# Softmax weights of layers 1 and 2: division by the sums moved from an activation into the product that turns them

## The chip, the cores and the metric

One Trainium2 chip, one of its cores. The metric is the device time of one launch in microseconds (us). The time of the kernel before is 1606.17 us, the median of 3 runs (1606.01 to 1606.25).

The engines of the core go by these names in the profile: PE (TensorE, matrix products; PEld is its loading of the stationary operand), ACT (ScalarE), DVE (VectorE), POOL (GpSimd) and SP (SyncE, which issues most of the DMA).

## The reference

The program computes, for 256 tokens of width 1024, two "hybrid" layers and then two layers of another block (gated feed-forwards, a neighbourhood attention with an mLSTM scan, a spatial gating). The change touches only the first two layers, and there the attention. Each layer has 16 heads of width 64: eight (group 0) with a causal mixture of three dilated windows, eight (group 1) with plain causal attention.

```python
def hybrid_layer(x, c, cos, sin, pre_g, post_g, w_ada, b_ada, w_in, w_out):
    shift, scale, gate = jnp.split(silu(c) @ w_ada + b_ada, 3, axis=-1)
    h = rms_norm(x, pre_g) * (1 + scale) + shift
    qa, ka, va, ga, qb, kb, vb, gb = jnp.split(h @ w_in, ...)
    ...
    o_a = merge(dilated_mixture_attention(qa, ka, va)) * silu(ga)   # softmax over causal windows
    o_b = merge(moba_attention(qb, kb, vb)) * silu(gb)              # softmax, causal
    y = concatenate([o_a, o_b]) @ w_out
    return x + gate * rms_norm(y, post_g)
```

For 256 tokens both attentions come down to, for each head, P = exp(S - max), each row divided by its own sum, and then P times V. The second block's first layer also has a context of 256 tokens, whose normalization (rms_norm of ctx, "cx0" in the kernel) is prepared at the end of layer 2.

## The kernel before, in words

Everything stays on the core. Weights stream from HBM in 428 tiles of 256 x 512; SP issues the transfers in an order fixed ahead, into a ring of slots. Each weight tile is split on the way into a high part (ACT, `act_tick`, a copy of 128x1024 to `sb_hi`) and a low part (DVE, `dve_tick`, a difference of 128x1024 to `sb_w..r`), and PE makes three products per tile and token block (high x high, high x low, low x high), each 128x512 or 128x256. Splits run three to seven tiles ahead of PE. DVE also makes the modulation vectors out of further tiles (`dve_vector`, 128x1024 each).

The order on each engine is written out by hand. Layer l has units u = 0 to 39, one weight tile each: q, k, v and q again of the two head groups, k, v, the gates (units 24 to 31), then the output projection (32 to 39). The table `B1` hangs further work on units: `("A", v)` and `("B", v)` are step v of the attention of group 0 and 1, and `("tq", g)`, `("tk", g)` are the turning of q and k. Step v of the attention does on PE (`pe_attention`) the following: turn head 2v-2 (`pe_turn`), weigh the two heads before (`pe_weigh`, P times V), scores of heads 2v and 2v+1 (`pe_scores`), turn head 2v-1. Steps lie about two units apart. A head's scores are 128x128 for its first 128 queries and 128x256 for its last.

The way of a pair of heads before the change is: PE scores into a bank; DVE adds the mask and finds the maxima (`dve_scores`); ACT takes the exponential, with the sum as its accumulator (`act_exp`, sums into `stat[..., 2:4]`); DVE takes the reciprocals of four sums at once (`dve_sums`, the item `"r"`); ACT multiplies the weights by them, in place, one 128x128 and one 128x256 activation for each head (`act_shares`); PE turns the three 128x128 blocks by transposes against the identity `ident` (`pe_turn`; it waits for the signal "share"); ACT copies the 128x384 out of the bank (`act_weights`); PE weighs.

POOL is nearly idle in these layers: it makes the 1/sqrt of the norms (`pool_rstd`, a power of -0.5 on one or two columns) and the low parts of some of the normalized rows (`pool_low`). `pool_norm(e, "cx0")` does so for the context. On DVE, `("cxn", i)` is the normalization of half i of the context and `("cx", i)` its further steps; PE turns it in `pe_norm(e, "cx0", ...)` when its own order comes to `("cx", i)`.

Of the kernel before, what the change touches and what calls it, by code (L numbers as in the profile page):

```python
# [353 lines left out]
def build(nc, I, out):  # L354
    ctx = ExitStack()
    with ctx:
# [64 lines left out]
        minus_half, kk2 = sb("minus_half", [128, 8]), sb("kk2", [128, 32])  # L421
        crow, ones = sb("crow", [1, 1024], at=xc_at), sb("ones", [1, 128], at=xc_at + 4096)
# [74 lines left out]
        def done(s, *what):  # L497
            return s, s.of(*what)
# [443 lines left out]
        def split_ready(*key):  # L942
# [12 lines left out]
              for g in range(2)]  # L955
        y = XN
# [17 lines left out]

        for v in range(4):
            for l in range(2):
                B1[l].setdefault(((16, 18, 20, 22), (11, 13, 15, 17))[l][v], []).insert(0, ("r", (0, v)))
                B1[l].setdefault(((25, 27, 29, 31), (23, 25, 27, 29))[l][v], []).insert(0, ("r", (1, v)))
# [142 lines left out]
        def pe_turn(e, l, g, h):  # L1121
            b = BANK["P", l, g, h] = HB3.take()
            for f in b.free():
                e.wait_ge(*f)
            e.wait_ge(*done(AE, "share", l, g, h))
            for x in range(3):
                m = e.tr(b.ap[:, x * 128:(x + 1) * 128], PB[h % 3][:, x * 128:(x + 1) * 128], ident)
            m.then_inc(TRP.sem, TRP.put("P", l, g, h))
            b.till = ((AE, "PT", l, g, h),)
# [37 lines left out]
        def act_shares(e, l, g, v):  # L1167

            e.wait_ge(*done(DE, "recip", l, g, v))
            for h in (2 * v, 2 * v + 1):  # L1170
                r, p = stat[:, l, g, h, :], PB[h % 3]
                e.act(p[:, 0:128], p[:, 0:128], ACT.Copy, scale=r[:, 2:3]).then_inc(AE.sem, AE.put("share", l, g, h, 0))
                e.act(p[:, 128:384], p[:, 128:384], ACT.Copy, scale=r[:, 3:4]).then_inc(AE.sem, AE.put("share", l, g, h))

# [34 lines left out]
        def dve_sums(e, l, g, v):  # L1209

            r = stat[:, l, g, 2 * v:2 * v + 2, 2:4]
            e.wait_ge(*done(EX, l, g, 2 * v + 1))
            e.recip(r, r).then_inc(DE.sem, DE.put("recip", l, g, v))
# [53 lines left out]
        def act_block1(e, l):  # L1267
# [18 lines left out]
            for u in range((35, 38)[l]):  # L1286
# [30 lines left out]
                for what, i in B1[l].get(u, ()):  # L1317
                    if what == "r":
                        act_shares(e, l, *i)
# [40 lines left out]
        def dve_block1(e, l):  # L1360
# [25 lines left out]
            for u in range((35, 38)[l]):  # L1386
                for what, i in B1[l].get(u, ()):
                    if what == "r":
                        dve_sums(e, l, *i)
# [100 lines left out]
        def pool_block1(e, l):  # L1490
            if l == 1:
                pool_rstd(e, "cx0")
                pool_norm(e, "cx0")
# [29 lines left out]

        def act_conditions(e):

            e.wait_ge(*done(LD["cb2"], 2))
            for n in range(4):
                c = slice(n % 2 * 512, n % 2 * 512 + 512)
                e.act(SG[n][:, :], CB[1 + n // 2][:, c], ACT.Tanh, scale=0.5).then_inc(AE.sem, AE.put("cb", 1 + n // 2, n % 2))

        def dve_conditions(e):

            for n in range(4):
                z = CB[1 + n // 2][:, n % 2 * 512:n % 2 * 512 + 512]
                e.wait_ge(*done(AE, "cb", 1 + n // 2, n % 2))
                e.stt(z, SG[n][:, :], 1.0, z, ALU.add, ALU.mult).then_inc(DE.sem, DE.put("cb", 1 + n // 2, n % 2))
# [42 lines left out]
        def pool_start(e):  # L1579
            e.memset(ones[:, :], 1.0).then_inc(PO.sem, PO.put("ones"))  # L1580
            e.memset(minus_half[:, :], -0.5).then_inc(PO.sem, PO.put("minus_half"))
            pool_rstd(e, "a0")
# [1523 lines left out]
```

## Time and profile before

| | |
|---|---|
| median of 3 runs | 1606.17 us (1606.01 to 1606.25) |
| the profiled execution | 1606.1 us, with a span of 1604.3 us from the first to the last instruction and 1.8 us around it |
| mean granted TensorE clock | 0.999 |
| PE busy | 1575.7 us, 98% of the span |
| PEld busy | 1311.9 us, 82% |
| DVE busy | 1173.6 us, 73% |
| ACT busy | 792.1 us, 49% |
| POOL busy | 70.4 us, 4% |

Times in the rows below are us from the start of the span. The attention of layer 1 lies between about 62 and 141 us, that of layer 2 between about 196 and 279 us. Durations of neighbouring matmuls overlap in the records, so for PE the distance from start to start is the time that a group takes.

### The profile page before, as it was taken

Reading aid. Unit: us, or ns where it says so; the run is one execution under the profiler, and the core shown is the slowest. Engines: PE = TensorE matmul, PEld = TensorE weight load, DVE = VectorE, ACT = ScalarE, POOL = GpSimd, SP = SyncE. Lnnn points to the kernel's source line nnn. Section 1 sums busy time; section 2 is a strip of 40 time slices with the busy share of each in tenths; the row PEclk is TensorE's granted clock in tenths of the full one; section 3 lists DMA queues with packets and bytes.
Section 4 is the critical chain, followed back from the end, with each engine's and each line's share of the span. In section 5 each row is a group of like instructions: output and inputs, shape, how many; then the busy total and the mean of one; then the engine's idle time right before and its main releaser. Section 6 shows DMA issues by size and latency. Waiting matters only on the chain.

```text
span 1604.3 us, 20979 instructions
## 1 busy us (share of the span) xinstructions
PE 1575.7 (98%) x8098; PEld 1311.9 (82%) x8098; DVE 1173.6 (73%) x1925; ACT 792.1 (49%) x1298; POOL 70.4 (4%) x112
## 2 busy tenths in 40 slices
PE   7999999999999999999999999999999999999998
PEld 5787778888888888887777888888888888888887
DVE  8899888759876665477755799868887667666654
ACT  5877677432221222254555555535554553455542
POOL 2000000100000000030010100000000100010000
PEclk9999999999999999999999999999999999999999
DMA  9987665336656664252131688766777585555550
GB/s 378 358 321 276 232 237 180 124 107 247 210 210 223 227 219 173 90 173 79 66 99 66 236 313 305 287 242 243 275 269 260 214 309 195 171 197 186 189 182 35
DMA packets 93046, 336.99 MB, mean 210 GB/s; under 512 B 10625, under 2 KB 11265, under 8 KB 92690
## 3 DMA queue, kind: packets, MB, share of 16 engines
q1 hardware_dynamic: 90706, 327.58, 56.6%
q0 software_dynamic: 2240, 8.06, 1.5%
q8 instruction: 64, 1.05, 0.3%
q14 instruction: 36, 0.29, 0.1%
HBM read 334.56 MB, written 1.05 MB: 209 GB/s over the span
## 4 chain that ended last, share of the span: by engine, by line
PE 54%; DVE 2%; issue 1%; ACT 0%; POOL 0%; POOLq 0%; DVEq 0%; ACTq 0%
PE bank L292 53%; PE bank L295 2%; DVE sb_tm L301 0%; DVE sb_XN L309 0%; DVE sb_XN L301 0%; DVE sb_X L301 0%; DVE sb_arena L312 0%; DVE sb_arena L319 0%; ACT sb_XN L298 0%; DVE sb_sg L316 0%; DVE sb_XC L301 0%; DVE sb_w8r L301 0%; DVE sb_w5r L301 0%; POOL sb_rstd L301 0%; DVE sb_arena L309 0%
## 5 line engine op out<-in xcount | busy, mean ns | idle before, releaser
L292 PE MATMUL bank<-sb_hT,sb_hi 128*128 128x512 f32 (+1 forms) x1856 | 574.7, 379 | 0.0
L298 ACT ACTIVATE sb_hi<-sb_w 128x1024 fp32r<-128x1024 f32 x428 | 432.0, 1052 | 286.1 <-DMA sb_w<-in_w 235.2
L292 PEld LDWEIGHTS bank<-sb_hT,sb_hi 128*128 128x128 f32 x1856 | 332.1, 188 | 58.5 <-issue 0.2
L292 PE MATMUL bank<-sb_hi,sb_hT 128*128 128x512 f32 x1152 | 369.6, 395 | 2.7 <-ACT sb_hT L298 1.3
L292 PEld LDWEIGHTS bank<-sb_hi,sb_hT 128*128 128x128 f32 x1152 | 215.6, 188 | 53.1 <-issue 5.3
L312 DVE CUSTOM_DVE_ANT_0 sb_w<-sb_w,sb_cb 128x1024 f32<-128x1024 f32 x144 | 174.9, 1219 | 0.0
L301 DVE TENSOR_TENSOR sb_sg<-bank,sb_sg 128x512 f32<-128x512 f32 (+1 forms) x90 | 58.8, 660 | 97.5 <-ACT sb_sg L298 78.0
L298 ACT ACTIVATE sb_sg<-bank 128x512 f32<-128x512 f32 (+1 forms) x98 | 55.0, 574 | 120.2 <-PE bank L292 120.0
L301 DVE TENSOR_TENSOR sb_tm<-bank,sb_rows 128x512 f32<-128x512 f32 (+1 forms) x41 | 28.1, 684 | 71.8 <-PE bank L292 68.9
L298 ACT ACTIVATE sb_arena<-bank 128x512 f32<-128x512 f32 (+1 forms) x106 | 56.2, 556 | 46.6 <-PE bank L292 32.5
L298 ACT ACTIVATE sb_XN<-sb_X 128x512 f32<-128x512 f32 x33 | 20.7, 629 | 99.7 <-DVE sb_X L301 92.7
L301 DVE TENSOR_TENSOR sb_w0r<-sb_w,sb_hi 128x1024 fp32r<-128x1024 f32 x43 | 52.3, 1217 | 18.6 <-ACT sb_hi L298 18.6
L301 POOL TENSOR_TENSOR sb_rstd<-sb_rstd,sb_minus_half 128x1 f32<-128x1 f32 (+1 forms) x23 | 14.1, 613 | 1174.7 <-DVE sb_rstd L309 1174.7
L298 ACT ACTIVATE sb_arena<-sb_arena,sb_stat 128x128 f32<-128x128 f32 (+1 forms) x128 | 52.2, 446 | 26.0 <-DVE sb_stat L312 26.0
L312 DVE CUSTOM_DVE_ANT_0 sb_w<-sb_w,sb_rows 128x1024 f32<-128x1024 f32 x48 | 57.7, 1221 | 0.3 <-ACT sb_rows L298 0.3
L301 DVE TENSOR_TENSOR sb_w3r<-sb_w,sb_hi 128x1024 fp32r<-128x1024 f32 x42 | 51.2, 1219 | 7.9 <-ACT sb_hi L298 7.7
L301 DVE TENSOR_TENSOR sb_w2r<-sb_w,sb_hi 128x1024 fp32r<-128x1024 f32 x39 | 47.8, 1226 | 10.7 <-ACT sb_hi L298 10.7
L301 DVE TENSOR_TENSOR sb_w1r<-sb_w,sb_hi 128x1024 fp32r<-128x1024 f32 x39 | 47.5, 1218 | 8.4 <-ACT sb_hi L298 8.4
L301 DVE TENSOR_TENSOR sb_w5r<-sb_w,sb_hi 128x1024 fp32r<-128x1024 f32 x36 | 43.9, 1220 | 10.2 <-ACT sb_hi L298 10.2
L312 DVE CUSTOM_DVE_ANT_0 sb_tmw<-sb_w,sb_cb 128x1024 f32<-128x1024 f32 x40 | 48.8, 1220 | 0.4
L295 PE MATMUL bank<-sb_cst,sb_arena 128*128 128x128 f32 x256 | 39.2, 279 | 8.6 <-ACT sb_arena L298 7.4
L292 PE MATMUL bank<-sb_hT,sb_w0r 128*128 128x256 f32 (+1 forms) x152 | 47.4, 321 | 0.0
(486 smaller groups left out, 3244.3 us busy)
## 6 DMA issues: line engine op xcount, KB each, us to landing
sb_w<-in_w SPq DMA_DIRECT2D x428, 512.0 KB, 4.3
sb_w<-in_mw SPq DMA_DIRECT2D x192, 512.0 KB, 4.9
sb_rows<-in_na_rpb POOLq DMA_DIRECT2D x16, 96.0 KB, 3.4
sb_X<-in_x SPq DMA_DIRECT2D x1, 1024.0 KB, 4.9
sb_cb<-in_cvec POOLq DMA_DIRECT2D x2, 512.0 KB, 9.4
sb_XC<-in_ctx POOLq DMA_DIRECT2D x1, 1024.0 KB, 13.2
sb_arena<-in_sg_ln_g POOLq DMA_DIRECT2D x1, 1024.0 KB, 5.9
sb_arena<-in_sg_ln_b POOLq DMA_DIRECT2D x1, 1024.0 KB, 9.1
```

What stands on the lines that cost most here:

```text
L292: return self.e.matmul(out, a, b, start=start, stop=stop)
L295: return self.e.transpose(out, a, ident)
L298: return self.e.activation(out, a, f, **kw)
L301: return self.e.tensor_tensor(out, a, b, op)
L312: return self.e.tensor_tensor_reduce(out=out, in0=a, in1=b, scale=scale, scalar=init, op0=op0, op1=op1, accum_out=accum)
```

## The change

Per pair of heads, the reciprocal leaves DVE and the two times two scaling activations leave ACT. In their place POOL raises the four sums to the power -1 (against a new constant `minus_one`), and then fills for each head a buffer `SHARE` of two 128x128 squares: the identity times the head's two columns of shares, that is, squares whose diagonal holds 1/sum (one for the first 128 queries, one for the last). `pe_turn` no longer transposes against `ident`; it multiplies each block of weights with its square, as an ordinary f32 product, so that the turned block comes out divided. `SHARE` has room for two heads and lies in `SG[3]`; a fill waits for the turn of the head two before. `SG[3]` was scratch for one of the four `tanh` of the conditions, which now uses half a row block of `XN`. Besides, the normalization of the context's second half, `("cxn", 1)`, moves from unit 34 to unit 33 of layer 2, and POOL's `pool_rstd(e, "cx0")` goes between the third and the fourth pair of group 0 in layer 2.

```diff
-               34: [("gate", 0), ("cxn", 1)], 35: [("cx", 2), ("cx", 3)]}]
+               33: [("cxn", 1)], 34: [("gate", 0)], 35: [("cx", 2), ("cx", 3)]}]
...
-        for v in range(4):
-            for l in range(2):
-                B1[l].setdefault(((16, 18, 20, 22), (11, 13, 15, 17))[l][v], []).insert(0, ("r", (0, v)))
-                B1[l].setdefault(((25, 27, 29, 31), (23, 25, 27, 29))[l][v], []).insert(0, ("r", (1, v)))
...
-            e.wait_ge(*done(AE, "share", l, g, h))
+            e.wait_ge(*done(PO, "share", l, g, h))
             for x in range(3):
-                m = e.tr(b.ap[:, x * 128:(x + 1) * 128], PB[h % 3][:, x * 128:(x + 1) * 128], ident)
+                m = e.mm(b.ap[:, x * 128:(x + 1) * 128], PB[h % 3][:, x * 128:(x + 1) * 128],
+                         SHARE[:, h % 2, min(x, 1), :], True, True)
...
-        def act_shares(e, l, g, v):
-
-            e.wait_ge(*done(DE, "recip", l, g, v))
-            for h in (2 * v, 2 * v + 1):
-                r, p = stat[:, l, g, h, :], PB[h % 3]
-                e.act(p[:, 0:128], p[:, 0:128], ACT.Copy, scale=r[:, 2:3]).then_inc(AE.sem, AE.put("share", l, g, h, 0))
-                e.act(p[:, 128:384], p[:, 128:384], ACT.Copy, scale=r[:, 3:4]).then_inc(AE.sem, AE.put("share", l, g, h))
...
-        def dve_sums(e, l, g, v):
+        def pool_shares(e, l, g, v):
 
             r = stat[:, l, g, 2 * v:2 * v + 2, 2:4]
             e.wait_ge(*done(EX, l, g, 2 * v + 1))
-            e.recip(r, r).then_inc(DE.sem, DE.put("recip", l, g, v))
+            e.tt(r, r, minus_one.rearrange("p (h j) -> p h j", h=2), ALU.pow).then_inc(PO.sem, PO.put("sums", l, g, v))
+            for h in (2 * v, 2 * v + 1):
+                if h > 1:
+                    e.wait_ge(*done(TRP, "P", l, g, h - 2))
+                elif g:
+                    e.wait_ge(*done(TRP, "P", l, 0, 6 + h))
+                e.wait_ge(*done(PO, "sums", l, g, v))
+                e.tt(SHARE[:, h % 2, :, :], ident.unsqueeze(1).to_broadcast([128, 2, 128]),
+                     stat[:, l, g, h, 2:4].unsqueeze(2).to_broadcast([128, 2, 128]), ALU.mult).then_inc(
+                    PO.sem, PO.put("share", l, g, h))
...
         def pool_block1(e, l):
+            e.wait_ge(*done(PO, "minus_one"))
+            for g in range(2):
+                for v in range(4):
+                    if (l, g, v) == (1, 0, 3):
+                        pool_rstd(e, "cx0")
+                    pool_shares(e, l, g, v)
             if l == 1:
-                pool_rstd(e, "cx0")
                 pool_norm(e, "cx0")
```

On PE, at the second step of the attention in layer 1 (`sb_arena` holds the weights, the scores' operands and the like; `sb_cst` is the identity, `sb_sg_85` is `SG[3]`, the squares; the moving operand is named first), before and now:

```order
 L292 MATMUL bank<-sb_hi_72,sb_hT 128x512
-L295 MATMUL bank<-sb_cst,sb_arena 128x128 x3
+L292 MATMUL bank<-sb_sg_85,sb_arena 128x128 x3
 L292 MATMUL bank<-sb_arena 128x128 x2
 L292 MATMUL bank<-sb_arena 128x256 x2
-L295 MATMUL bank<-sb_cst,sb_arena 128x128 x3
+L292 MATMUL bank<-sb_sg_85,sb_arena 128x128 x3
 L292 MATMUL bank<-sb_hi_73,sb_hT 128x512
```

Each group of three transposes has become three products in the same place; nothing else has moved on PE. There are 32 such groups, 96 instructions.

On POOL, in layer 2, between the end of layer 1's low parts (`sb_hT`) and the power for the context (`sb_rstd`, 128x2), and behind it:

```order
 L301 TENSOR_TENSOR sb_hT<-sb_sg_85,sb_hT 128x2x128
+L301 TENSOR_TENSOR sb_stat<-sb_stat,sb_minus_one 128x2x2
+L301 TENSOR_TENSOR sb_sg_85<-sb_cst,sb_stat 128x256 x2
...
 L301 TENSOR_TENSOR sb_rstd<-sb_rstd,sb_minus_half 128x2
+L301 TENSOR_TENSOR sb_stat<-sb_stat,sb_minus_one 128x2x2
+L301 TENSOR_TENSOR sb_sg_85<-sb_cst,sb_stat 128x256 x2
```

POOL's queue has gained, over both layers, 16 powers of four columns and 32 fills of 128x256, in this pattern.

On DVE, at the end of layer 2 (`sb_XN<-sb_XC` is the normalization of the context's second half, the others are low parts of weight tiles):

```order
 L301 TENSOR_TENSOR sb_w0r<-sb_w_49,sb_hi_75 128x1024
 L301 TENSOR_TENSOR sb_w8r<-sb_w_65,sb_hi_76 128x1024
+L305 TENSOR_SCALAR sb_XN<-sb_XC,sb_rstd 128x512 x2
 L301 TENSOR_TENSOR sb_w1r<-sb_w_51,sb_hi_71 128x1024
 L301 TENSOR_TENSOR sb_w4r<-sb_w_57,sb_hi_72 128x1024
-L305 TENSOR_SCALAR sb_XN<-sb_XC,sb_rstd 128x512 x2
```

It now stands two low parts earlier. ACT has lost 64 activations and DVE 16 reciprocals; both keep the order of the rest.

## Rows read from the trace of the kernel before

**Rows 1.** The page: span and busy time of each engine

```profile
span 1604.3 us, 20979 instructions
PE 1575.7 (98%) x8098; PEld 1311.9 (82%) x8098; DVE 1173.6 (73%) x1925; ACT 792.1 (49%) x1298; POOL 70.4 (4%) x112
```

**Rows 2.** Waits of PE, 0 to 330 us: total us, times, longest

```profile
PE bank L295 <- ACT sb_arena L298: 7.4, 11, 1.6
```

**Rows 3.** Timeline of PE: turns that waited (start, us, idle before)

```profile
70.31 0.52 PE L295 MATMUL bank<-sb_cst,sb_arena 128*128 128x128 f32 x3 [0.16 <-ACT sb_arena L298]
...
135.62 0.52 PE L295 MATMUL bank<-sb_cst,sb_arena 128*128 128x128 f32 x3 [1.17 <-ACT sb_arena L298]
...
218.53 1.39 PE L295 MATMUL bank<-sb_cst,sb_arena 128*128 128x128 f32 x11 [0.45 <-ACT sb_arena L298]
...
274.29 0.52 PE L295 MATMUL bank<-sb_cst,sb_arena 128*128 128x128 f32 x3 [1.32 <-ACT sb_arena L298]
```

**Rows 4.** Timeline of PE: eight transposes and the product behind them

```profile
183.13 1.04 PE L295 MATMUL bank<-sb_cst,sb_arena 128*128 128x128 f32 x8
183.92 0.48 PE L292 MATMUL bank<-sb_hi,sb_hT 128*128 128x512 f32 x1
```

**Rows 5.** Timeline of PE: eight f32 products (16 records), mLSTM stage

```profile
764.75 1.95 PE L292 MATMUL bank<-sb_arena,sb_tm 128*128 128x128 f32 x16
766.45 0.48 PE L292 MATMUL bank<-sb_hi,sb_hT 128*128 128x512 f32 x1
```

**Rows 6.** Timeline of PE: eight f32 products against the identity (gate rows)

```profile
140.92 2.05 PE L292 MATMUL bank<-sb_cst,sb_mods 128*128 128x128 f32 x16
142.73 0.47 PE L292 MATMUL bank<-sb_hi,sb_yT0h 128*128 128x512 f32 x1
```

**Rows 7.** Groups of POOL with shapes: busy us, mean ns, idle before

```profile
L301 POOL TENSOR_TENSOR sb_hT<-sb_sg,sb_hT 128x256 fp32r<-128x256 f32 x28 | 21.8, 778 | 61.9 <-ACT sb_hT L298 61.9
L301 POOL TENSOR_TENSOR sb_rstd<-sb_rstd,sb_minus_half 128x1 f32<-128x1 f32 x20 | 11.1, 553 | 1121.4 <-DVE sb_rstd L309 1121.4
L301 POOL TENSOR_TENSOR sb_mlhr<-sb_mlhr,sb_minus_half 128x8 f32<-128x8 f32 x1 | 1.7, 1674 | 0.1
```

**Rows 8.** Timeline of DVE and POOL: one power alone, one beside DVE

```profile
217.13 0.70 POOL L301 TENSOR_TENSOR sb_rstd<-sb_rstd,sb_minus_half 128x2 f32<-128x2 f32 x1 [44.27 <-DVE sb_rstd L309]
...
686.57 1.22 DVE L301 TENSOR_TENSOR sb_w1r<-sb_w,sb_hi 128x1024 fp32r<-128x1024 f32 x1
686.73 1.63 POOL L301 TENSOR_TENSOR sb_rstd<-sb_rstd,sb_minus_half 128x2 f32<-128x2 f32 x1 [2.17 <-DVE sb_rstd L309]
```

**Rows 9.** Timeline of DVE and POOL around 290 us

```profile
289.29 1.52 POOL L301 TENSOR_TENSOR sb_hT<-sb_sg,sb_hT 128x512 fp32r<-128x512 f32 x1 [71.46 <-ACT sb_hT L298]
290.19 1.70 DVE L301 TENSOR_TENSOR sb_w8r<-sb_w,sb_hi 128x1024 fp32r<-128x1024 f32 x1 [0.51 <-ACT sb_hi L298]
```

**Rows 10.** Timeline of ACT and DVE: exponentials' ends, and one pair's neighbours

```profile
67.38 0.19 ACT L298 ACTIVATION_READ_ACCUMULATOR sb_arena<-sb_arena,sb_stat 128x1 f32 x1
...
132.21 0.19 ACT L298 ACTIVATION_READ_ACCUMULATOR sb_arena<-sb_arena,sb_stat 128x1 f32 x1
134.68 1.49 ACT L298 ACTIVATE sb_arena<-sb_arena,sb_stat 128x128 f32<-128x128 f32 x4
...
269.62 0.19 ACT L298 ACTIVATION_READ_ACCUMULATOR sb_arena<-sb_arena,sb_stat 128x1 f32 x1
...
132.15 1.22 DVE L312 CUSTOM_DVE_ANT_0 sb_w<-sb_w,sb_rows 128x1024 f32<-128x1024 f32 x1
133.38 1.19 DVE L301 TENSOR_TENSOR sb_w3r<-sb_w,sb_hi 128x1024 fp32r<-128x1024 f32 x1
```

**Rows 11.** Groups of DVE, 55 to 332 us

```profile
L322 DVE RECIPROCAL sb_stat<-sb_stat 128x4 f32<-128x4 f32 x16 | 2.8, 177 | 6.7 <-ACT sb_arena L298 6.7
```

**Rows 12.** Timeline of PE: first turn of the context's second half

```profile
294.71 1.29 PE L295 MATMUL bank<-sb_cst,sb_XN 128*128 128x128 f32 x8 [1.14 <-DVE sb_XN L305]
```

**Rows 13.** Windows: us, then busy time (instructions) of PE, PEld, DVE, ACT, POOL

```profile
120.00:140.00 20.00, 17.22 (x123) 14.27 (x121) 19.17 (x41) 15.38 (x39) 0.00 (x0) 1.00 0.77 285
```

More of the change, by code:

```diff
@@ L421, in build @@
         minus_half, kk2 = sb("minus_half", [128, 8]), sb("kk2", [128, 32])
+        minus_one = sb("minus_one", [128, 4])
         crow, ones = sb("crow", [1, 1024], at=xc_at), sb("ones", [1, 128], at=xc_at + 4096)
@@ L955, in build @@
               for g in range(2)]
+        SHARE = SG[3].rearrange("p (h j c) -> p h j c", h=2, j=2)
         y = XN
@@ L1316, in act_block1 @@
                         act_norm(e, "cx0", 0, cx_free(), (i,))
-                for what, i in B1[l].get(u, ()):
-                    if what == "r":
-                        act_shares(e, l, *i)
             act_edge1(e, l)
@@ L1386, in dve_block1 @@
             for u in range((35, 38)[l]):
-                for what, i in B1[l].get(u, ()):
-                    if what == "r":
-                        dve_sums(e, l, *i)
                 if (l, u) != (0, 34):
@@ L1522, in act_condition, with condition @@
                 AE.sem, AE.put("cb", *((0,) if nh else (0, nh))))
+        def condition(n):
+            return XN[:, 0, 512:1024] if n == 3 else SG[n][:, :]
         def act_conditions(e):
@@ L1528, in act_conditions @@
                 c = slice(n % 2 * 512, n % 2 * 512 + 512)
-                e.act(SG[n][:, :], CB[1 + n // 2][:, c], ACT.Tanh, scale=0.5).then_inc(AE.sem, AE.put("cb", 1 + n // 2, n % 2))
+                e.act(condition(n), CB[1 + n // 2][:, c], ACT.Tanh, scale=0.5).then_inc(AE.sem, AE.put("cb", 1 + n // 2, n % 2))
         def dve_conditions(e):
@@ L1535, in dve_conditions @@
                 e.wait_ge(*done(AE, "cb", 1 + n // 2, n % 2))
-                e.stt(z, SG[n][:, :], 1.0, z, ALU.add, ALU.mult).then_inc(DE.sem, DE.put("cb", 1 + n // 2, n % 2))
+                e.stt(z, condition(n), 1.0, z, ALU.add, ALU.mult).then_inc(DE.sem, DE.put("cb", 1 + n // 2, n % 2))
         def dve_start(e):
@@ L1581, in pool_start @@
             e.memset(minus_half[:, :], -0.5).then_inc(PO.sem, PO.put("minus_half"))
+            e.memset(minus_one[:, :], -1.0).then_inc(PO.sem, PO.put("minus_one"))
             pool_rstd(e, "a0")
```

## The prediction

> **What bounds the kernel now.** I read the page first. PE is busy for 98% of a span of 1604.3 us, DVE for 73%, ACT for 49%, POOL for 4% [rows 1]. An engine that is never idle for long sets the time, so an edit is worth what it does to PE: the length of PE's own instructions, and the moments in which PE stands still. Everything that ACT, DVE and POOL gain or lose counts only through those moments.
>
> Then the waits, of PE alone and up to 330 us, where layers 1 and 2 lie. The largest item is 7.4 us in 11 waits, of a transpose for something that ACT wrote into the arena [rows 2]. In the timeline these are the turns of the weights; they wait for the scaled weights [rows 3]. One of the 11, of 0.45 us, stands before a group of eleven transposes, of which eight turn k and come first; it does not belong to the weights and stays. The change can take away the rest, 6.9 us. It cannot take away more there, because the other 22 groups find their weights ready.
>
> So the question is whether PE's new products cost less than 6.9 us over the old transposes, and whether POOL delivers in time.
>
> **PE: 96 transposes become 96 f32 products.** The trace has both forms at the same size, and between the same neighbours, products of 128x512. Eight transposes take from 183.13 to 183.92, 0.79 us, 0.099 each [rows 4]. Eight f32 products of 128x128 by 128x128, which show as 16 records, take from 764.75 to 766.45, 1.70 us, 0.2125 each [rows 5]. A product costs 0.114 us more, and 96 x 0.114 = **+10.9 us**. A second place, eight products against the identity, gives 1.81 us, 0.226 each [rows 6], 0.127 more and +12.2 us in sum. I take the first, because there the stationary operand is a full block of data as here; 12.2 is the upper end. This is work on the engine that bounds, and nothing hides it. The two record counts say why: one record for a transpose, two for a product.
>
> By the Trainium skill, page "FP8 and Floating Point Precision", section "TensorE Precision Notes", a true f32 product takes four passes through the array, and by "TensorE: Matmul & The Clock Gate", section "Terms", the transpose mode is four times faster for f32. Worked out from these pages, as an estimate, the factor would be four where the rows show 0.2125 / 0.099 = 2.1; with the product's 0.2125 kept, the sum would be 96 x 0.16 = 15.3 us. The rows decide, and the sum keeps 10.9.
>
> **PE: waits for the shares.** Gone: **-6.9 us**. What comes instead is POOL's chain: the last exponential, a power on four columns, a fill, and the turn. The fill has a near row, 128x256 with two inputs, 0.78 us [rows 7]. The power of four columns has none: one column takes 0.553, eight take 1.674 [rows 7]; between them, 0.16 a column, four take 1.03. With 0.1 for each of two signals the first square is there 2.0 us after the last exponential if POOL runs alone.
>
> It does not run alone. A power of two columns took 0.70 us by itself, and 1.63 when it started 0.16 us behind a DVE difference of 128x1024 that ran until 687.79 [rows 8]: POOL's read came only after the end of DVE's. The other way round, a DVE difference took 1.70 us instead of 1.22 [rows 8] when it started while POOL was at work on 128x512 until 290.81 [rows 9]. So each of the two engines waits for the other's whole instruction. That holds for DVE's instructions with two inputs in SBUF, and DVE runs these of 1.2 us back to back in the attention. So the power and the first fill can each lose up to 1.1 us, and the second fill, behind which DVE has queued up in the meantime, about 1.15.
>
> The Trainium skill has this as a rule ("SBUF — State Buffer", section "Who interferes with whom"): a DVE instruction with two SBUF inputs and a GpSimd instruction that reads SBUF exclude each other for a whole instruction. The trace agrees, with the 1.63 and the 1.70 above.
>
> One pair worked out, the last of layer 1: its last sum is there at 132.21 + 0.19 = 132.40, DVE is busy until 133.37 [rows 10]; the power ends at about 134.4, DVE's next ends at 134.57 and the fill at 135.35, with the signal 135.4. PE comes to the turn at 135.62 - 1.17 = 134.45 [rows 3]. It would wait 0.9 us, where it waited 1.17 because ACT's scaling (134.68) stood behind other copies [rows 10]. I laid the same over all 16 pairs, from the first (sums 67.57, turn 70.15) to the last (sums 269.81, turn 272.97) [rows 3, 10], with DVE's instructions where they stand; most pairs leave 2.5 to 4 us, and the new waits add up to **+2.3 us** in four pairs. Without any exclusion they are 0; with a power of 1.6 us, as eight columns take, they are 9.1. Those are the bounds, and the row for the fill is close enough to stay by 2.3.
>
> **ACT and DVE.** ACT loses 64 activations, DVE 16 reciprocals of 0.18 us and 6.7 us in which it stood before them waiting for the exponentials [rows 11]. PE waits for neither otherwise, so this is worth 0 by itself. DVE pays for the fills: 32 times about 0.65 us of exclusion, up to 21 us. In the tightest stretch DVE is busy for 19.17 of 20 us [rows 13]. It gets back 9.5 us from the reciprocals, and PE itself becomes 10.9 us longer there, which is time for DVE too; together 20.4. I set 0, as the low parts run some tiles ahead of PE; the price if that cover goes is in the second rival.
>
> **The context's norm a tile ahead.** PE waits 1.14 us for it at 294.71 [rows 12]. Two low parts of 128x1024, 1.22 us each [rows 8], stood before it that now stand behind, 2.4 us: **-1.1 us**. What is late next are those two low parts, by the short time of two normalizations, and PE needs them some tiles later. POOL's power for the context, moved ahead among the pairs, is made long before its use.
>
> **The sum.** +10.9 - 6.9 + 2.3 - 1.1 = +5.2 us against the profiled execution's 1606.1, which lies 0.07 under the median: **1611.3 us**, 0.32% slower. Own range of this case: lowest 10.9 - 6.9 + 0 - 1.1 = +2.9 (1609.0), highest 12.2 - 6.9 + 9.1 = +14.4 with nothing from the context (1620.5); the likely part is 1609 to 1615.
>
> **Rivals.**
> 1. POOL is the one waited for. The power costs 1.6 us or more, or each step loses a whole DVE instruction. Waits of 9.1 instead of 2.3: +12, 1618. For it: the exclusion in rows 8 and DVE's dense queue. Against it: most turns come 2.5 us or more after the exponentials.
> 2. DVE falls behind. If the exclusion is as dear as 21 us and comes in stretches such as that with 0.83 us to spare in 20 [rows 13], PE waits for low parts; I put it at two whole low parts of DVE, 2.4 us less the 0.83 to spare, about 1.5 us in each of the four groups of eight heads: +5.2 + 6 = +11, 1617. Against it: PE's own lengthening gives DVE room.
> 3. No measurable change (within 0.2%, 3.2 us, about what a measurement of this kernel can tell): all old waits go, the relief of ACT and DVE removes further small ones, no new ones come. That is +2.9 or a little less, 1609.
> 4. Faster. The mechanism would be that a product of these blocks costs what a transpose costs, for instance if loading the block set the pace of both. Then -6.9 + 2.3 - 1.1 = -5.7, 1600.4. It decides against me if a product costs less than 0.026 us more than a transpose (96 x 0.026 = 2.5, and 5.7 - 2.5 = 3.2). Rows 5 and 6, two places that agree within 7%, speak against it. For it there is only that neither is this very product.
>
> **How the numbers follow.** My forecast, +3.2 to +8: 0.53. Rival 1: 0.15. Rival 2: 0.11. Rival 3: 0.14. Rival 4: 0.07. Slower is the sum of the first three, 0.79; same 0.14; faster 0.07. The range: below, rival 4 (0.07) and the lower half of rival 3 are left out, so 1608; above, it takes in both slow rivals at their worked-out prices, 1617 and 1618, and leaves what is beyond: 1619.
>
> **What the profile afterwards would show.** The groups of three as products that take about 0.64 us together (3 x 0.2125), where three transposes at 0.099 take 0.30; PE's busy time up by some 11 us. Waits of PE for POOL's squares in a few pairs, 2 us in sum, and none for ACT's shares. Powers near 1.0 us and fills near 0.8 when DVE is idle, both up to 2 when it is not. DVE differences of 1.22 us stretched to 1.7 or so beside fills. No wait at the context's turn. I am wrong if the products start closer than 0.15 us apart, or if PE waits for POOL in most pairs.

## The result, and the profile after

The changed kernel takes 1611.62 us (median of 6 runs, 1611.44 to 1612.58) where the kernel before takes 1606.11 us in the same comparison (6 runs, 1605.84 to 1606.53). The ratio is 1.0035, with a 95% interval of 1.0022 to 1.0048: slower by a third of a per cent, 0.3 us from the forecast.

The page of the profiled execution of the changed kernel, its head and the busy times of the engines:

```profile
span 1610.7 us, 21166 instructions
PE 1587.0 (99%) x8194; PEld 1324.9 (82%) x8194; DVE 1182.8 (73%) x1909; ACT 771.1 (48%) x1234; POOL 125.8 (8%) x161
```

Against [rows 1] the span is 6.4 us longer. PE is busy for 11.3 us more and idle for 4.9 us less (28.6 before, 23.7 now), which is the whole of it. This execution took 1612.58 us, the longest of the six and 1.0 above their median, so the sums taken from its trace can be about 1 us too high. ACT lost 21 us of work, which by itself gave PE nothing. DVE shed 16 reciprocals, 2.8 us, and is still busy for 9.2 us more: about 12 us of stretch in its other instructions.

PE in the timeline of the changed kernel: start, duration, instruction. A group of three products shows as six records.

```profile
79.15 0.83 PE L292 MATMUL bank<-sb_sg,sb_arena 128*128 128x128 f32 x6
79.91 1.73 PE L292 MATMUL bank<-sb_arena 128*64 128x256 f32 x16
81.56 0.94 PE L292 MATMUL bank<-sb_sg,sb_arena 128*128 128x128 f32 x6
82.25 0.48 PE L292 MATMUL bank<-sb_hi,sb_hT 128*128 128x512 f32 x1
```

From start to next start the first group takes 0.76 us and the second 0.69. Half of the 32 groups take 0.69 and the others 0.76 to 0.84, 0.74 on average, where the three transposes before took 0.30 to 0.45.

PE's waits in the changed kernel up to 340 us, those in the attention and at the weights: us in total, times, longest.

```profile
PE bank L292 <- POOL sb_sg L301: 2.1, 3, 1.0
...
PE bank L295 <- DVE sb_arena L301: 1.0, 2, 0.7
PE bank L295 <- DVE sb_XN L305: 0.7, 1, 0.7
PE bank L292 <- DVE sb_w2r L301: 0.6, 1, 0.6
PE bank L292 <- DVE sb_w5r L301: 0.5, 1, 0.5
```

The row of [rows 2], 7.4 us in 11 waits for ACT, is gone. In its place stands POOL, 2.1 us in three waits. These three in the timeline, and the context's turn of [rows 12], which now has no wait behind it:

```profile
98.51 0.91 PE L292 MATMUL bank<-sb_sg,sb_arena 128*128 128x128 f32 x6 [0.98 <-POOL sb_sg L301]
...
138.38 0.91 PE L292 MATMUL bank<-sb_sg,sb_arena 128*128 128x128 f32 x6 [0.95 <-POOL sb_sg L301]
...
263.55 0.91 PE L292 MATMUL bank<-sb_sg,sb_arena 128*128 128x128 f32 x6 [0.21 <-POOL sb_sg L301]
...
301.34 1.03 PE L295 MATMUL bank<-sb_cst,sb_XN 128*128 128x128 f32 x8
```

POOL's new instructions by line (duration in ns: least, median, most; first and last start; shapes):

```profile
L301 POOL TENSOR_TENSOR sb_sg<-sb_cst,sb_stat x32: 612/644/1597, 70.4 to 280.3; 128x256 f32<-128x256 f32 x32
...
L301 POOL TENSOR_TENSOR sb_stat<-sb_stat,sb_minus_one x16: 1342/1354/1760, 68.6 to 278.2; 128x4 f32<-128x4 f32 x16
```

A fill that nothing holds up takes 0.61 us, against 0.78 forecast. The power shows 1.35 us or more against 1.03, but each of the 16 ran beside a DVE instruction; what that means stands below under "The exclusion". From the end of the last sum to the end of the first square it is 2.2 us in eleven pairs and 2.6 in the other five, where the forecast had 2.0 for POOL alone.

### The profile page after: what moved, and what is told of

Same layout as the page of the kernel before. It is cut to its first block, busy times and chain, and to the rows that moved or that the text cites. A ratio compares the mean times of both kernels' runs of the same rounds, so it can differ in the third digit from the quotient of the medians.

```text
span 1610.7 us, 21166 instructions
## 1 busy us (share of the span) xinstructions
PE 1587.0 (99%) x8194; PEld 1324.9 (82%) x8194; DVE 1182.8 (73%) x1909; ACT 771.1 (48%) x1234; POOL 125.8 (8%) x161
## 3 DMA queue, kind: packets, MB, share of 16 engines
q8 instruction: 65, 1.06, 0.3%
## 4 chain that ended last, share of the span: by engine, by line
PE 54%; DVE 2%; issue 1%; ACT 0%; POOL 0%; POOLq 0%; DVEq 0%; ACTq 0%
PE bank L292 53%; PE bank L295 2%; DVE sb_tm L301 0%; DVE sb_XN L309 0%; DVE sb_XN L301 0%; DVE sb_X L301 0%; DVE sb_arena L312 0%; DVE sb_arena L319 0%; ACT sb_XN L298 0%; DVE sb_sg L316 0%; DVE sb_XC L301 0%; DVE sb_w8r L301 0%; DVE sb_w5r L301 0%; POOL sb_rstd L301 0%; DVE sb_arena L309 0%
## 5 line engine op out<-in xcount | busy, mean ns | idle before, releaser
L301 DVE TENSOR_TENSOR sb_w4r<-sb_w,sb_hi 128x1024 fp32r<-128x1024 f32 x31 | 38.3, 1234 | 10.7 <-ACT sb_hi L298 10.7
L301 DVE TENSOR_TENSOR sb_w8r<-sb_w,sb_hi 128x1024 fp32r<-128x1024 f32 x32 | 40.4, 1261 | 7.2 <-ACT sb_hi L298 7.2
```

Source lines behind the costliest of these rows:

```text
L301: return self.e.tensor_tensor(out, a, b, op)
```

## The experiments

By the sum of the prediction everything fitted. But a total of four terms can be right while the terms are not, so they were done alone, undone, or doubled. Medians are in us; each ratio is to the kernel before, timed on the same chip in the same job (its medians there: 1605.93 to 1606.19).

| run | what it is | median | ratio, 95% interval |
|---|---|---|---|
| e1_transposes | after, with transposes | 1608.15 | 1.0012 (1.0003 to 1.0021) |
| e2_products_alone | before, with products | 1613.01 | 1.0042 (1.0029 to 1.0056) |
| e3_norm_alone | before, with the norm a tile ahead | 1604.52 | 0.9990 (0.9981 to 0.9999) |
| e4_no_power | after, without the powers | 1610.08 | 1.0026 (1.0016 to 1.0036) |
| e5_pool_scales | POOL scales the weights in place | 1623.34 | 1.0107 (1.0092 to 1.0122) |
| e6_more_fills | after, with 64 fills more | 1624.39 | 1.0113 (1.0096 to 1.0130) |
| e7_products_norm | before, with products and norm | 1611.16 | 1.0032 (1.0020 to 1.0043) |
| e8_shares_first | e3, with ACT's scaling first | 1613.11 | 1.0042 (1.0028 to 1.0056) |
| e9_two_pairs | e3, with squares for two pairs | 1603.79 | 0.9988 (0.9979 to 0.9997) |
| e10_products_twice | after, each product twice | 1629.11 | 1.0143 (1.0127 to 1.0158) |

### e1: transposes in place of the products

```diff
-                m = e.mm(b.ap[:, x * 128:(x + 1) * 128], PB[h % 3][:, x * 128:(x + 1) * 128],
-                         SHARE[:, h % 2, min(x, 1), :], True, True)
+                m = e.tr(b.ap[:, x * 128:(x + 1) * 128], PB[h % 3][:, x * 128:(x + 1) * 128], ident)
```

> The changed kernel with the three f32 products of each turn put back to transposes against the identity. POOL's powers and fills and PE's wait for them stay; what is left out is the division of the weights by their sums, since nothing uses the squares. Theory (the products cost 0.12 us more each on the engine that bounds): 96 x 0.12 = 11.5 us less than the changed kernel, about 1600, which is 6 us under the kernel before, with PE's waits for POOL near 2 to 3 us as in the changed kernel. Rival (the time went to the exclusion between POOL and DVE, and products are nearly free): within 2 us of the changed kernel, 1610 to 1612.

Measured: 1608.15 us (10 runs, 1607.15 to 1609.09, gathered around 1607.2 and 1609.0). The turns became short again, yet the time fell by only 3.5 us, and not to the 1600 of the expectation's theory; its rival, 1610 to 1612, missed too. The page and PE's row for POOL in the waits:

```profile
PE 1577.4 (98%) x8098; PEld 1313.4 (82%) x8098; DVE 1182.8 (74%) x1909; ACT 770.5 (48%) x1234; POOL 125.8 (8%) x161
...
PE bank L295 <- POOL sb_sg L301: 6.4, 6, 2.4
```

PE's busy time fell by 9.6 us, but its waits for POOL rose from 2.1 to 6.4. So POOL's way is hardly better, as seen by PE, than ACT's was (6.9 for the weights): it looks short in the changed kernel because PE comes later there. The expectation had it worth 2 to 3 us of wait with either kind of turn, and it missed. (The busy time would have fallen by more; part of it is TensorE's clock, see the last section.)

### e2: products against the identity, nothing else

```diff
-                m = e.tr(b.ap[:, x * 128:(x + 1) * 128], PB[h % 3][:, x * 128:(x + 1) * 128], ident)
+                m = e.mm(b.ap[:, x * 128:(x + 1) * 128], PB[h % 3][:, x * 128:(x + 1) * 128], ident, True, True)
```

> The kernel before with one edit: the 96 transposes of the weights are f32 products against the identity. ACT scales and DVE takes reciprocals as before, so the computation is complete. Theory (products cost 0.12 us more each): before + 10.9 to 12 us, less up to 1 us of old waits that the longer products cover, so 1616 to 1618. Rival (products nearly free): 1606 to 1608.

Measured: 1613.01 us. The page and PE's row for ACT:

```profile
PE 1587.7 (99%) x8194; PEld 1325.3 (82%) x8194; DVE 1174.1 (73%) x1925; ACT 792.3 (49%) x1298; POOL 70.4 (4%) x112
...
PE bank L292 <- ACT sb_arena L298: 2.2, 5, 0.9
```

PE is busy for 12.0 us more, 0.125 us a product. And the wait for ACT's shares falls from 7.4 us in 11 to 2.2 us in 5, though ACT and DVE do what they did. The longer turns cover 5.2 us of it by themselves. The expectation, 1616 to 1618, had allowed 1 us for this and missed.

### e3: the context's norm a tile ahead, nothing else

```diff
-               34: [("gate", 0), ("cxn", 1)], 35: [("cx", 2), ("cx", 3)]}]
+               33: [("cxn", 1)], 34: [("gate", 0)], 35: [("cx", 2), ("cx", 3)]}]
```

> The kernel before with one edit: the normalization of the context's second half a unit earlier (33 instead of 34). Theory: PE's wait of 1.14 us before the context's last turns goes, and nothing comes for it: 1605.0 against 1606.1. Rival: the two low parts behind which DVE is now late, or the turns' later steps, take it back: 1606.1.

Measured: 1604.52 us, 1.6 less. PE's waits of this kernel:

```profile
PE bank L295 <- ACT sb_arena L298: 7.4, 11, 1.6
...
PE bank L295 <- DVE sb_XN L305: 0.7, 1, 0.7
```

The row of 7.4 us is as before, and the wait at the context's turn (1.14 us, [rows 12]) is gone; what is left for `sb_XN` is another turn's 0.7.

### e7: products and norm, the division left with ACT and DVE

The two edits of e2 and e3 together. Added up, their differences give 1606.1 + 6.9 - 1.6 = 1611.4.

> The kernel before with two edits: f32 products against the identity in the turns, and the context's norm a unit earlier. ACT still scales the weights and DVE takes the reciprocals, so against the changed kernel only POOL's part is missing; the computation is complete. Theory (longer turns alone cover most of the old waits, and the move of the division to POOL is worth nothing more): products alone gave 1613.0, the norm alone -1.6, so 1611.4, equal to the changed kernel. Rival (POOL's squares are what removed the old waits): at least 3 us above the changed kernel, 1614.5 or more.

Measured: 1611.16 us (6 runs, 1611.06 to 1611.74), against 1611.62 for the whole change; the intervals of the two ratios overlap. Page and PE's row for ACT:

```profile
PE 1587.5 (99%) x8194; PEld 1325.4 (82%) x8194; DVE 1174.2 (73%) x1925; ACT 792.5 (49%) x1298; POOL 70.5 (4%) x112
...
PE bank L292 <- ACT sb_arena L298: 2.2, 5, 0.9
```

This kernel divides as before, with ACT's 64 activations and DVE's 16 reciprocals, and it takes the time of the changed one. The move of the division to POOL, which is what the change is about, brings no gain that can be measured: the medians differ by 0.5 us, in favour of ACT. 2.2 us of wait for ACT are given for 2.1 us of wait for POOL.

### e4: no powers

```diff
-            e.tt(r, r, minus_one.rearrange("p (h j) -> p h j", h=2), ALU.pow).then_inc(PO.sem, PO.put("sums", l, g, v))
...
-                e.wait_ge(*done(PO, "sums", l, g, v))
```

> The changed kernel without POOL's 16 powers: the squares are filled with the sums themselves instead of their reciprocals, so the weights are multiplied by their sums (the division is left out). Each square is ready 1.35 us or more sooner. Theory (PE waits for POOL's chain of power and fill in the three pairs with the least room): the 2.1 us of waits go, 1609.5 against 1611.6. Rival (these waits are set by the exclusion with DVE alone, so that the fill ends when DVE's instruction lets it whatever comes before): less than 1 us.

Measured: 1610.08 us, 1.5 less than the changed kernel. (The intervals of the two ratios overlap, but eight of the nine runs lie below the lowest run of the changed kernel.) No row of PE's waits names POOL any more. A wait for a low part of a weight tile grew in its place, from 0.6 to 1.2 us:

```profile
PE bank L292 <- DVE sb_w2r L301: 1.2, 1, 1.2
```

So the wait for POOL costs the changed kernel about what its row of 2.1 us says, less what is late next.

### e5: POOL scales the weights in place, and PE transposes

The turns are those of e1; the other part of the edit is this.

```diff
-                e.tt(SHARE[:, h % 2, :, :], ident.unsqueeze(1).to_broadcast([128, 2, 128]),
-                     stat[:, l, g, h, 2:4].unsqueeze(2).to_broadcast([128, 2, 128]), ALU.mult).then_inc(
+                p = PB[h % 3]
+                e.tt(p[:, 0:128], p[:, 0:128], stat[:, l, g, h, 2:3].to_broadcast([128, 128]), ALU.mult).then_inc(
+                    PO.sem, PO.put("share", l, g, h, 0))
+                e.tt(p[:, 128:384], p[:, 128:384], stat[:, l, g, h, 3:4].to_broadcast([128, 256]), ALU.mult).then_inc(
```

> POOL multiplies the weights in place by their shares (one 128x128 and one 128x256 per head, as ACT did before the change), behind the same power; the turns are transposes again, and the context's norm stays a unit earlier. The computation is complete. Theory (products 11 us, old waits 6.9, norm 1.1): no cost on PE, so 1606.1 - 6.9 - 1.1 + the waits for POOL, whose chain is longer than with squares (about 1.1 us of work per head instead of 0.62, and twice the exclusion): some 3 to 7 us of waits, 1601 to 1605. Rival (POOL in the chain is itself the loss): above 1607.

Measured: 1623.34 us, where 1601 to 1605 was expected. PE's waits:

```profile
PE bank L295 <- POOL sb_arena L301: 18.2, 15, 3.7
```

Four instructions for each pair instead of two, each of which may have to let a DVE instruction pass, and turns that are short again: 15 of the 32 turns now wait. The theory that POOL could take the division off everybody's hands without products fell.

### e6: more fills

Behind each fill two more of 128x128 into a buffer of their own, for which nobody waits. It asks for rival 2: is DVE the one that runs late when POOL does more?

```diff
+                e.wait_ge(PO, PO.n)
+                e.tt(junk[:, :], ident, stat[:, l, g, h, 2:3].to_broadcast([128, 128]), ALU.mult).then_inc(
+                    PO.sem, PO.put("twice", l, g, h, 0))
+                e.wait_ge(PO, PO.n)
+                e.tt(junk[:, :], ident, stat[:, l, g, h, 3:4].to_broadcast([128, 128]), ALU.mult).then_inc(
+                    PO.sem, PO.put("twice", l, g, h, 1))
```

> The changed kernel with two further fills of 128x128 behind each fill, into scratch that nobody waits for: 64 more POOL instructions that read SBUF, so about double the time in which POOL and DVE exclude each other. Theory (DVE has enough room, and PE waits for POOL only where a pair is short of time): the second square of a pair comes about 0.8 us later, 1 to 4 us more waits, 1612.5 to 1616. Rival (DVE is at its limit and already costs part of the 5.5 us): PE waits for DVE's low parts, 6 us or more, above 1618.

Measured: 1624.39 us. The expectation missed: the fills of a pair's first head stand ahead of the fill of its second, and that one is waited for. PE's waits:

```profile
PE bank L292 <- POOL sb_sg L301: 12.7, 9, 2.4
...
PE bank L292 <- DVE sb_w5r L301: 0.9, 1, 0.9
...
PE bank L292 <- DVE sb_w2r L301: 0.3, 1, 0.3
```

It answers a part of the question. Even with three POOL instructions where one stood, PE's waits for DVE's low parts stay at 0.9 and 0.3 us (0.5 and 0.6 in the changed kernel), so the price that rival 2 named isn't paid. That DVE doesn't run late doesn't follow: PE, standing 12.7 us for POOL, gives DVE time, and before the turn at 99.09 the last sum came 0.53 us ahead of PE, where it came 1.35 ahead in the changed kernel and 2.27 in e2. How that comes about stands below under "The new waits". The extra fills are also drawn out by DVE, so the size of the harm is not the price of 64 short instructions.

### e8: ACT's scaling at the head of its unit

ACT's scaling of [rows 10] stood behind other copies; here it comes first in its unit, on top of e3.

```diff
+                for what, i in B1[l].get(u, ()):
+                    if what == "r":
+                        act_shares(e, l, *i)
...
-                for what, i in B1[l].get(u, ()):
-                    if what == "r":
-                        act_shares(e, l, *i)
```

> The kernel before with the context's norm a unit earlier, and ACT's scaling of the weights at the head of its unit, ahead of that unit's split of a weight tile and its copies out of banks, instead of behind them. The turns are transposes, the computation is complete. Theory (the old waits come from ACT's own queue: the sums are there, the scaling stands behind 1 to 3 us of other work): PE's waits for the scaled weights fall from 7.4 to 2 to 4 us, 1604.5 - 4 = 1600 to 1602. Rival (the reciprocal on DVE is what is late, and ACT now also stands and waits for it): no gain, 1604 to 1607.

Measured: 1613.11 us, 8.6 more than e3. The waits of PE and ACT in this kernel:

```profile
PE bank L295 <- ACT sb_arena L298: 9.2, 9, 2.3
...
PE bank L295 <- DVE sb_arena L301: 2.6, 1, 2.6
...
ACT sb_arena L298 <- DVE sb_stat L322: 7.7, 14, 1.1
```

ACT comes to the scaling before DVE has made the reciprocals, and stands 7.7 us in 14 waits with its copies of weight tiles behind it. In the old order the copies ahead of the scaling filled that time. This order does not win the old waits back; it adds to them. The theory (1600 to 1602) fell, and the rival had the mechanism right and the price (1604 to 1607) too low. The traced execution took 1611.73, the shortest of the five: 7.2 of span more than e3's, 5.5 of it idle time of PE and 1.7 busy time, which is the clock again (last section).

### e9: squares only for the two pairs that waited longest

On top of e3, POOL makes the squares for two of the sixteen pairs, those whose turns at 126 and 274 us waited longest; the others stay with ACT and transposes.

```diff
+        SQUARES = ((0, 1, 2), (1, 1, 3))
...
+            squares = (l, g, h // 2) in SQUARES
+            e.wait_ge(*done(PO if squares else AE, "share", l, g, h))
...
+                if squares:
+                    m = e.mm(b.ap[:, x * 128:(x + 1) * 128], p, SHARE[:, h % 2, min(x, 1), :], True, True)
+                else:
+                    m = e.tr(b.ap[:, x * 128:(x + 1) * 128], p, ident)
```

> The kernel before with the context's norm a unit earlier, and the change's way (POOL's power and squares, products in the turns) for two of the 16 pairs only: the third pair of group 1 in layer 1 and the last of group 1 in layer 2, before which PE waited 1.61 and 1.32 us. The other 14 pairs keep ACT's scaling and transposes. The computation is complete. Theory (squares pay where the old wait is larger than the products' 6 x 0.12 us, since the changed kernel shows no wait at these two pairs): 1604.5 - 2.9 + 1.4 = 1603.0. Rival (the waits have moved by then, or another pair inherits them): 1604.5 to 1606.

Measured: 1603.79 us (11 runs, eight of them within 1603.53 to 1603.88 and three at 1605.2 to 1605.7), the fastest of all, 0.12% below the kernel before and 0.5% below the changed one. Its interval overlaps that of e3 (1604.52), so that the squares' own part, 0.7 us, is not proven. PE's row for ACT, and the turn at 135 us:

```profile
PE bank L295 <- ACT sb_arena L298: 5.1, 9, 1.9
...
135.46 0.52 PE L295 MATMUL bank<-sb_cst,sb_arena 128*128 128x128 f32 x3 [1.86 <-ACT sb_arena L298]
```

2.3 us of wait went and twelve products came, but a neighbour that kept ACT's way, the turn at 135 us, waits 1.86 where it waited 1.17 [rows 3]: 0.7 us of what was taken away came back there.

### e10: every product twice

The disputed cost by itself: the same kernel with 96 products more.

```diff
-            for x in range(3):
+            for x in (0, 1, 2, 0, 1, 2):
```

> The changed kernel with each of the 96 products made twice into the same place, the computation is complete. Theory (a product costs PE about 0.21 us, and the changed kernel has few waits left to cover it): 96 x 0.2125 = 20.4 us more, less the 2 to 3 us of waits that it covers, 1629 to 1632. Rival (products overlap with their neighbours and cost what transposes do, 0.1): 1621 or less.

Measured: 1629.11 us, 17.5 more. The page:

```profile
span 1627.2 us, 21550 instructions
PE 1607.6 (99%) x8386; PEld 1346.6 (83%) x8386; DVE 1183.0 (73%) x1909; ACT 771.4 (47%) x1234; POOL 126.8 (8%) x161
```

PE's busy time grew by 20.6 us, 0.2146 us for each of the 96, within 1% of the 0.2125 from [rows 5]. (From start to start, a group of 0.69 became one of 1.36, which is 0.223 for each product added.) The span grew by only 16.5. 3.1 us of the rest are waits that vanish: no row of PE's waits names POOL any more (2.1 before), and the two for `sb_arena` (1.0) are gone too.

## Why the prediction was right, point by point

The forecast time, 1611.3, came out within 0.3 us, and each term stands in the changed kernel's own trace at about its size. Two of the reasons behind the terms were wrong. That this didn't show in the total is luck: the first error touches only how the terms are shared out between the parts of a change that has both parts, and in the second two errors cancel.

**The products: +10.9 forecast.** PE is busy for 11.3 us more with the change, 12.0 in e2, and e10 gives 0.2146 us a product. The row from the layers behind, 8 products in 1.70 us, was a fair price for products in another place. What the sum needed is the difference to a transpose. In the attention a group of three products takes 0.74 us on average and one of three transposes took 0.36, where 0.64 and 0.30 were forecast; the difference is 0.125 a product instead of 0.114. Rival 4, a product at the price of a transpose, falls. The Trainium skill's factor of four between an f32 product and a transpose ("TensorE: Matmul & The Clock Gate", section "Terms") doesn't show here: by e10 and [rows 4] it is 0.2146 / 0.099 = 2.2.

**The old waits: -6.9 forecast.** They did go. (The wait of 0.45 us before the turning of k, which was to stay, did stay, as 0.71 for DVE.) The reason given was wrong: "the change can take away the rest" credited the division's new place with all of it, and "nothing hides it" put the products at their full length. By e2 longer turns alone cover 5.2 us, and e7, with products and the division where it was, takes the time of the changed kernel within the measurement. The step that failed is that the waits and the length of the turns were put down as two independent terms. The right account is: products +10.9 to 12, of which the old waits give back 5.2, so +6.9 measured in e2; the norm -1.6; POOL in place of ACT between 0 and +0.5. How longer turns cover the waits can be read at a turn that e2 shares with the kernel before (first line before, second e2):

```profile
126.19 0.52 PE L295 MATMUL bank<-sb_cst,sb_arena 128*128 128x128 f32 x3 [1.61 <-ACT sb_arena L298]
127.82 0.91 PE L292 MATMUL bank<-sb_cst,sb_arena 128*128 128x128 f32 x6 [0.47 <-ACT sb_arena L298]
```

PE came to it at 124.58 and in e2 at 127.35, 2.8 us later, while the scaled weights were there only 1.6 later. At the turns of 135.62 and 274.29 PE came 2.4 and 6.4 later and the weights 1.6 and 6.0. So PE is put off by more than ACT's queue is; why ACT's queue is put off by less is not shown. e10, where POOL's waits vanish as the turns grow once more, and e1, where they rise from 2.1 to 6.4 as the turns shrink, go with that. e1 and e3 both have transposes and the moved norm; in e3 ACT scales the weights, in e1 PE waits for POOL's squares, though nothing uses them. PE is idle for 27.9 us in e1 and 27.4 in e3. So POOL's division saves PE no waiting with short turns either.

**The new waits: +2.3 forecast, in four pairs.** 2.1 us in three. The size was right and its parts were not. All three are waits for the first square of a pair. The forecast let the power and the first fill lose up to 1.1 us each; the power lost less (below) and the first fill nothing, so that the chain is shorter than was worked out, 2.6 us instead of 3.0 in the last pair of layer 1. But the forecast kept the time between the last sum and PE's turn as it was, and that became shorter. It is 1.35, 1.78 and 2.11 us in the three pairs, where e2, with the same long turns and no work on POOL, has 2.27, 2.84 and 2.79. With e2's room the chain of 2.2 to 2.6 and its signal of 0.1 would have fitted, but for less than 0.1 us. The lines of the first of the three, in the changed kernel and in e2, show where the time went: the turn behind which the scores stand, and DVE's first instruction on these scores.

```profile
88.69 0.83 PE L292 MATMUL bank<-sb_sg,sb_arena 128*128 128x128 f32 x6
93.26 0.28 DVE L312 CUSTOM_DVE_ANT_0 sb_arena<-bank,sb_arena 128x128 f32<-128x128 f32 x1
...
88.11 0.83 PE L292 MATMUL bank<-sb_cst,sb_arena 128*128 128x128 f32 x6
92.05 0.29 DVE L312 CUSTOM_DVE_ANT_0 sb_arena<-bank,sb_arena 128x128 f32<-128x128 f32 x1
```

DVE comes to the scores 4.57 us behind that turn instead of 3.94, without having been idle before them; in the other two pairs it comes 1.0 and 0.8 us later in the same sense. It had been drawn out by the fills of the pair before. So late scores make late sums, and PE's wait, which the trace puts down to POOL, is in good part DVE's lateness. This is read from traces; no run takes the fills' hold on DVE away by itself. The waits are worth about what they say: without powers the kernel is 1.5 us faster (e4).

**The exclusion.** It is there, and here it can be seen. DVE and POOL in the timeline of the changed kernel:

```profile
95.52 1.22 DVE L301 TENSOR_TENSOR sb_w2r<-sb_w,sb_hi 128x1024 fp32r<-128x1024 f32 x1
96.26 1.35 POOL L301 TENSOR_TENSOR sb_stat<-sb_stat,sb_minus_one 128x4 f32<-128x4 f32 x1 [7.82 <-ACT sb_arena L298]
96.66 1.22 DVE L312 CUSTOM_DVE_ANT_0 sb_w<-sb_w,sb_rows 128x1024 f32<-128x1024 f32 x1
97.75 2.16 POOL L301 TENSOR_TENSOR sb_sg<-sb_cst,sb_stat 128x256 f32<-128x256 f32 x2
97.81 1.64 DVE L312 CUSTOM_DVE_ANT_0 sb_w<-sb_w,sb_rows 128x1024 f32<-128x1024 f32 x1
```

The two fills, of 0.61 us each when nothing holds them up, took 2.16: the first 0.61, the second 1.59. The DVE instruction that began just behind the first took 1.64 instead of 1.22. PE's turn at 98.51 had waited 0.98 us for the first of them. Of the 16 second fills twelve took 1.59 or 1.60, two 1.06 and two 0.61; no first fill took more than 0.67.

The power's 1.35 us is not its own price. It ended at 97.61, 0.87 behind the end of the DVE instruction that was running when it began (96.74). Another power began earlier beside its DVE instruction:

```profile
135.40 1.22 DVE L312 CUSTOM_DVE_ANT_0 sb_w<-sb_w,sb_rows 128x1024 f32<-128x1024 f32 x1
135.73 1.75 POOL L301 TENSOR_TENSOR sb_stat<-sb_stat,sb_minus_one 128x4 f32<-128x4 f32 x1 [6.88 <-ACT sb_arena L298]
```

It took 1.75 and ended at 137.48, 0.86 behind the end of that one (136.62). All 16 powers end 0.86 to 0.92 us behind such an end, eleven of them after 1.34 to 1.36 us and five after 1.73 to 1.76. So the power waits too. By [rows 8] a power of two columns took 0.70 alone and ended 0.57 behind DVE's end when it was held up, 0.13 less; with the same 0.13 a power of four would take about 1.0 alone. That is an estimate, and it bears out the forecast's 1.03. The loss is then about 0.35 us in eleven pairs and 0.75 in five. The Trainium skill has the exclusion as a rule ("SBUF — State Buffer", section "Who interferes with whom"); the 1.64 and the 2.16 agree with it, and so do the powers.

**DVE: 0 forecast.** The same group of DVE in the stretch from 60 to 145 us, before and after (busy us, mean ns of one | idle before):

```profile
L312 DVE CUSTOM_DVE_ANT_0 sb_w<-sb_w,sb_rows 128x1024 f32<-128x1024 f32 x28 | 33.6, 1220 | 0.0
```

```profile
L312 DVE CUSTOM_DVE_ANT_0 sb_w<-sb_w,sb_rows 128x1024 f32<-128x1024 f32 x28 | 36.1, 1309 | 0.0
```

Each costs 0.09 us more on average, and all of DVE about 12 us of the 21 that were the bound. PE's waits for low parts hardly grew (`sb_w2r` 0.3 to 0.6, `sb_w5r` 0.6 to 0.5). But 0 was not the right term for DVE: its stretch is paid for in the late scores above, and before the turning of k at 223.56, where PE waited 0.71 us for DVE. The work that DVE does there, before and after:

```profile
217.15 0.78 DVE L301 TENSOR_TENSOR sb_tm<-sb_arena,sb_rcs 128x256 f32<-128x256 f32 x2
221.89 1.07 DVE L301 TENSOR_TENSOR sb_tm<-sb_arena,sb_rcs 128x256 f32<-128x256 f32 x2
```

Beside it POOL was making two squares and the context's power, which the change had put there. Rival 2 had the stretch right and named the wrong work of DVE as what PE would wait for.

**The norm: -1.1 forecast.** -1.6 us in the time of e3, -1.1 in its waits (1.8 to 0.7); the 0.5 between them is within what the comparison resolves. Nothing came late behind it that PE had to wait for.

**Rival 1** (POOL waited for, 1618) was right that the steps lose time to DVE's instructions, though the first fill lost none, and its price of 9 us was wrong: the late turns of PE leave POOL room, and e1 shows what the same chain costs, 6.4 us, when they don't. **Rival 3** (no change, 1609) needed no new waits at all; e4 comes nearest, 1610.08.

## What to carry to other kernels

On an engine that is 98% busy, a wait and the length of the instructions ahead of it are not two terms: longer work covers part of the wait, whatever else is done to end it. So before a wait is credited to the edit that removes it, ask how much of it would go if only the engine's own instructions grew, and test that with the one-line kernel that does it. Of a change made of parts, keep the part that is paid for: here the one-line move of the norm (and perhaps squares for the two worst pairs), which is faster than both kernels, while 96 longer products buy waits that cost less than they do. And a wait for one engine can be another's fault: when POOL is given work that holds DVE up, look at what DVE makes for the same chain, and compare when each step's inputs arrive, not only who is named last.

## What the hardware showed that was not expected

PE's clock fell in the middle of the dense part. In e1, PE stood still for 2.40 us before 97.11 and for 2.14 us before 136.49:

```profile
97.11 0.52 PE L295 MATMUL bank<-sb_cst,sb_arena 128*128 128x128 f32 x3 [2.40 <-POOL sb_sg L301]
...
136.49 0.54 PE L295 MATMUL bank<-sb_cst,sb_arena 128*128 128x128 f32 x3 [2.14 <-POOL sb_sg L301]
```

The windows behind the second (us from start, length, busy us of PE, PEld, DVE, ACT, POOL, then PE's granted clock, the share of DMA and GB/s):

```profile
136.40:138.00 1.60, 1.51 (x9) 0.98 (x11) 1.60 (x3) 1.15 (x2) 1.50 (x1) 0.65 1.00 356
138.00:140.00 2.00, 2.00 (x12) 1.48 (x9) 2.00 (x3) 0.49 (x1) 0.00 (x0) 0.50 0.96 360
140.00:142.00 2.00, 2.00 (x10) 1.67 (x9) 2.00 (x4) 1.06 (x1) 0.00 (x0) 0.93 1.02 401
142.00:144.00 2.00, 2.00 (x17) 1.33 (x16) 2.00 (x4) 0.55 (x1) 0.00 (x0) 1.00 0.80 279
```

The granted clock was 0.65 and then 0.50, the lower of its two levels, 1.2 of 2.4 GHz, until past 140 us, and PE's busy time in all is 1.7 us above that of the kernel before, with the same instructions. The record has the low level from 136.87 for 3.4 us, and half of that is the 1.7. Behind the longer wait at 97.11 the clock stayed at 1.00, so a fall doesn't follow every such wait. e8 shows the same once, for 3.4 us from 224.4 behind a wait of 2.62 us; e5 for 6.8 us from 101.0 and 3.4 from 145.4, behind waits of 3.69 and 2.85; and e6 for 6.8 us from 100.6, behind one of 1.80. So some 5 us of e5's loss and up to 3.4 of e6's are this. In the changed kernel, whose longest wait in the attention is 0.98 us, the clock is 1.00 throughout it. The runs of e1, e8 and e9 gather around two times 1.5 to 1.8 us apart, and the longer ones show a mean granted clock lower by 0.001; that fits, but of each only one execution was traced, so it is not shown.

No run has POOL's power of four columns with DVE idle, so its own price is only the estimate above, near 1.0 us, between 0.55 for one column and 1.67 for eight [rows 7]. A fill with two broadcast inputs (0.61 us when nothing holds it up) is a little faster than a product of full ones of the same size (median 0.74).
